# Weight-block sums of the first feed-forward product: from VectorE to GpSimd

## Chip, cores and metric

One core of a Trainium2 chip. The metric is the device time of one execution in microseconds (us); "before" is the median of three runs. The core has TensorE (matrix products), VectorE (DVE in the rows), ScalarE (ACT), GpSimd (POOL) and SyncE (SP, here the queue that issues the loads). TensorE's matmul is PE in the rows, its weight load PEld.

## The reference, cut to what matters

The whole model is two transformer blocks in float32 on 512 tokens of 1024 values. The change touches only the last stage, the feed-forward network of the second block:

```python
def squared_relu_mlp(u, w_ff1, w_ff2):          # u: 512 x 1024, w_ff1: 1024 x 4096, w_ff2: 4096 x 1024
    hdn = jnp.square(jax.nn.relu(jnp.einsum('bld,df->blf', u, w_ff1)))
    return jnp.einsum('blf,fd->bld', hdn, w_ff2)
```

Ahead of it stand the mixer's output projection (w_out), its residual sum and a root-mean-square norm; behind it a residual sum and the final norm.

## The kernel before

**Float32 products from split halves.** A float32 operand is kept as a hi half (rounded by a copy on ScalarE) and a lo half (the rest, a subtraction on VectorE, the helper `rest`, L2059). A product is three matmuls: hi with hi, hi with lo, lo with hi (`mm3`, L614 to L616).

**Units.** The 4096 hidden columns are handled in 16 units of 256 columns, in 4 groups (NFF) of 4. A unit of kind "one" (s = 0 to 15) makes 256 hidden columns; a unit of kind "two" makes 256 output columns from the 1024 hidden columns of one group. The order `SEQ` is: the four "one" units of group 0; then for each further group, alternately "one" of that group and "two" of the group before; last the four "two" units of group 3.

**The first product with seven block products.** A unit "one" is not multiplied straight. The weights of 1024 x 256 are seen as blocks 11, 12, 21, 22 (`squares_of`), the tokens as two halves, and 7 products take the place of 8 (the Strassen-Winograd form). Three of the seven take weight blocks as they are (tiles a and d of a ring), four take sums of blocks: 21+22, that minus 11, 11-21, 12 minus the second. These four sums (tile `sums`, four parts of 128x512) are what the change is about. Before, VectorE makes them in `left_sums` (L2725, L2726, L2727, L2729). ScalarE then copies them to hi halves in two pairs (`s_hi`, L1962), and VectorE makes the lo halves in two pairs (`left_lo`, parts 1 and 2). Part 0 of `left_lo` is the lo half of a and d. TensorE takes the products in the order 1, 2, 6, 5, 7, 3, 4: products 1 and 2 need part 0, 6 and 5 need part 1, 7 and 3 need part 2 (`unit_one`); product 4 takes d.

**Buffers.** Raw weights (1 MB a unit) land in two slots, `raw`, alternating over SEQ. Split halves and sums of a "one" unit lie in a ring: `ring_first` for unit 0, `ring_odd` for units 1 and 3, `ring_even` for all others. So units 1 to 4 have their ring free when product 4 of the unit before the last is done (unit 1: when w_out's last tile is done), while from unit 5 on the ring is free only when product 4 of the unit just before is done. The four sums share their memory with the lo halves `s_lo`. The SyncE queue issues the load of a slot once the splits that read it are done: before, for a "one" unit, after part 0 of `left_lo`.

**VectorE's order, written by hand.** In group 0, in the turn of unit s: first sum of product results (L2784), `left_sums(s+1)`, `left_lo(s+1, 0)`, middle sums (L2790, L2792), lo halves of the hidden tiles of unit s-1, `left_lo(s+1, 1)` and `(s+1, 2)`, last sum (L2797) and the square of the positive part (two scalar_tensor_tensor, L2801). After unit 3 the norm's reciprocal (L2079) and its square. From group 1 on: L2784, `two_lo` (lo halves of a "two" unit), middle sums, hidden lo halves, L2797, L2801, then `left_sums(s+1)` and all of `left_lo(s+1)`, then the residual sums of two "two" tiles (L2820, L2822). ScalarE has a matching order. The last matmul of each product signals `pe_done`; `done(eng, label)` waits for it. GpSimd has no work in the kernel.

The semaphores are counted: `sums_ready` twice a unit before; `w_lo_ready` three times for a "one" unit (`W_AT` holds the base).

Of the kernel before, what the change touches and what calls it, by code (L numbers as in the profile page):

```python
# [25 lines left out]
ALU = mybir.AluOpType  # L26
# [5 lines left out]
KT = D // P  # L32
# [4 lines left out]
RAW = 2  # L37
# [17 lines left out]
NFF = 4  # L55
# [22 lines left out]
U0 = {}  # L78
# [48 lines left out]
SEQ = [("one", 0, u) for u in range(4)]  # L127
# [4 lines left out]
SEQ_AT = {_x: _j for _j, _x in enumerate(SEQ)}  # L132
SPLITS = {"one": 3, "two": 2}
W_AT = [U0["ffn"]]
# [19 lines left out]
def build(nc, t, out):  # L154
    with ExitStack() as ctx:
# [51 lines left out]
        one = vecs[:, NVEC + 1:NVEC + 2]  # L207
# [139 lines left out]
        raw_in = [sem(f"raw_in{i}") for i in range(RAW)]  # L347
# [3 lines left out]
        w_lo_ready = sem("w_lo_ready")  # L351
# [117 lines left out]
        sums_ready = sem("sums_ready")  # L469
# [17 lines left out]
        block = ctx.enter_context(nc.Block())  # L487
# [23 lines left out]
        def odd(s):  # L511
            return s < 4 and s % 2 == 1

        def ring_of(s):
            return ring_first if s == 0 else ring_odd if odd(s) else ring_even
# [10 lines left out]
        def squares_of(u):  # L526

            x = raw[:, u % RAW, :].rearrange("p (i o n) -> p i o n", i=4, o=2)
            return {"a": x[:, :, :, 0:P], "11": x[:, :, 0, 0:P], "12": x[:, :, 1, 0:P],
                    "21": x[:, :, 0, P:2 * P], "22": x[:, :, 1, P:2 * P]}  # L530
# [998 lines left out]
        def done(eng, label):  # L1529

            eng.wait_ge(pe_done, marks.at[label])
            return marks.banks.get(label)


        @block.scalar
        def _(act):
            def split_hi(u):
# [53 lines left out]
            for i in range(4):  # L1591
                u = U0["conv"] + 3 * i
# [363 lines left out]
            def left_sums(s):  # L1956

                r = ring_of(s)
                for i in range(2):
                    act.wait_ge(sums_ready, 2 * s + i + 1)  # L1960
                    c = slice(2 * i, 2 * i + 2)
                    act.activation(r["s"][0][:, c, :, :], r["sums"][:, c, :, :], ACT.Copy).then_inc(w_hi_ready, 1)  # L1962

# [48 lines left out]
            for s in range(4 * NFF):  # L2012
                g, u = divmod(s, 4)
# [34 lines left out]
        def _(dve):  # L2048
            steps = [0]

            def link(ins):

                steps[0] += 1
                ins.then_inc(dve_step, 1)
                dve.wait_ge(dve_step, steps[0])
# [48 lines left out]
            for m in range(KT):  # L2104
                dve.wait_ge(u_hi_ready, m + 1)
                dve.scalar_tensor_tensor(out=C_lo[:, m, :], in0=X[:, m, :], scalar=vec("norm_mix_g", m),  # L2106
                                         in1=C_hi[:, m, :].bitcast(F32), op0=ALU.mult, op1=ALU.subtract)\
# [7 lines left out]
            def latent(m, dst):  # L2115
# [12 lines left out]
                                   in1=vecs[:, g0:g0 + KT].unsqueeze(2).broadcast_to([P, KT, META]), op=ALU.mult))  # L2128
            dve.tensor_tensor(out=meta[:, :, :], in0=meta[:, :, :],
                              in1=meta_sq[:, 0, :].unsqueeze(1).broadcast_to([P, KT, META]), op=ALU.mult)\  # L2130
# [6 lines left out]
            for i in range(4):  # L2137
                u = U0["conv"] + 3 * i
                split_lo(u + 2)
                if i == 0:  # L2140
                    dve.wait_ge(lat_std_ready, 1)
                    link(dve.reciprocal(rstd[:, :], std[:, :]))
                    for k in range(2):
                        dve.scalar_tensor_tensor(out=cqn[:, k, :], in0=cqn[:, k, :], scalar=vec("q_norm_g", k),
                                                 in1=rstd[:, :], op0=ALU.mult, op1=ALU.mult).then_inc(lat_ready, 1)
# [133 lines left out]
            for k in range(KT):  # L2279
                dve.scalar_tensor_tensor(out=memx[:, k, :], in0=memx[:, k, :], scalar=vec("norm_memkv_g", k),  # L2280
                                         in1=rstd[:, 0:MEM], op0=ALU.mult, op1=ALU.mult).then_inc(mem_n_ready, 1)
# [62 lines left out]
            for i in range(4):  # L2344
# [12 lines left out]
                if i < 2:  # L2357
# [8 lines left out]
                                   in1=rstd_t[:, :].unsqueeze(2).broadcast_to([P, TT, EXPERTS]), op=ALU.mult))  # L2366
            link(dve.reduce_max(mx[:, 0:TT], lg, AX_X))
            dve.tensor_tensor(out=aff[:, :, :], in0=lg, in1=mx[:, 0:TT].unsqueeze(2).broadcast_to([P, TT, EXPERTS]),
                              op=ALU.subtract).then_inc(logit_ready, 1)
# [4 lines left out]
                              in1=ri[:, 0:TT].unsqueeze(2).broadcast_to([P, TT, EXPERTS]), op=ALU.mult)\  # L2374
# [8 lines left out]
            for i in range(CAP // 8):  # L2383
# [3 lines left out]
                if i + 1 < CAP // 8:  # L2387
# [9 lines left out]
                              in1=picked[:, :, :], op=ALU.mult).then_inc(pos_ready, 1)  # L2397
# [28 lines left out]
            for p in range(EPAIRS):  # L2426
# [17 lines left out]
                for half in range(2):  # L2444
# [3 lines left out]
                                             in1=YO_hi[:, c].bitcast(F32), op0=ALU.mult, op1=ALU.subtract)\  # L2448
# [72 lines left out]
            for i in range(2):  # L2521
# [5 lines left out]
                              in1=vecs[:, g0:g0 + 2].unsqueeze(2).broadcast_to([P, 2, META]), op=ALU.add)\  # L2527
# [20 lines left out]
            for c in range(2):  # L2548
                dve.wait_ge(z_copied, Z[f"a{4 * c + 3}"])
                for g in (2 * c, 2 * c + 1):  # L2550
# [3 lines left out]
                    for j in range(g + 1):  # L2554
                        dst = win[:, j % 2, :]
                        link(dve.tensor_tensor(out=dst[:, 2 * n - 1:TOK], in0=src[:, 2 * n - 1:TOK],
                                               in1=src[:, n - 1:TOK - n], op=ALU.add))
                        src, n = dst, 2 * n
                    dve.scalar_tensor_tensor(out=AA[:, g, META:TOK], in0=src[:, META:TOK], scalar=1.0 / n,
                                             in1=AA[:, g, META:TOK], op0=ALU.mult, op1=ALU.subtract)\  # L2560
# [10 lines left out]
            for g in range(4):  # L2571
# [3 lines left out]
                                         in1=PH_hi[:, g, :].bitcast(F32), op0=ALU.mult, op1=ALU.subtract)\  # L2575
# [32 lines left out]
            for i in range(4):  # L2608
# [12 lines left out]
                              in0=b[:, :, :, CHUNK - 1:CHUNK].broadcast_to([P, 2, S // CHUNK, CHUNK]), in1=b,  # L2621
                              op=ALU.subtract).then_inc(kd_sub, 1)
            dve.tensor_tensor(out=KD[:, :, 0:META],
                              in0=B2[:, :, META - 1:META].broadcast_to([P, 2, META]), in1=B2[:, :, 0:META],
                              op=ALU.subtract).then_inc(kd_sub, 1)
# [89 lines left out]

            def left_sums(s):

                u = U0["ffn"] + SEQ_AT[("one", s // 4, s % 4)]
                dve.wait_ge(raw_in[u % RAW], 16 * (u // RAW + 1))
                if s == 1:  # L2720
                    done(dve, ("w_out", KT - 1))
                elif s:
                    done(dve, ("p", s - 2 if s < 5 else s - 1, 4))
                x, d = squares_of(u), ring_of(s)["sums"]
                link(dve.tensor_tensor(out=d[:, 0, :, :], in0=x["21"], in1=x["22"], op=ALU.add))  # L2725
                dve.tensor_tensor(out=d[:, 1, :, :], in0=d[:, 0, :, :], in1=x["11"], op=ALU.subtract).then_inc(sums_ready, 1)  # L2726
                dve.tensor_tensor(out=d[:, 2, :, :], in0=x["11"], in1=x["21"], op=ALU.subtract)  # L2727
                dve.wait_ge(sums_ready, 2 * s + 1)
                dve.tensor_tensor(out=d[:, 3, :, :], in0=x["12"], in1=d[:, 1, :, :], op=ALU.subtract).then_inc(sums_ready, 1)  # L2729

            def left_lo(s, part):

                j = SEQ_AT[("one", s // 4, s % 4)]
                r = ring_of(s)
                dve.wait_ge(w_hi_ready, W_AT[j] + part + 1)
                if part == 0:
                    x = squares_of(U0["ffn"] + j)
                    rest(r["a"][1][:, :, :, :], x["a"], r["a"][0][:, :, :, :])
                    rest(r["d"][1][:, :, :], x["22"], r["d"][0][:, :, :]).then_inc(w_lo_ready, 1)
                    return  # L2740
                c = slice(2 * part - 2, 2 * part)
                dve.wait_ge(sums_ready, 2 * s + 2)
                rest(r["s"][1][:, c, :, :], r["sums"][:, c, :, :], r["s"][0][:, c, :, :]).then_inc(w_lo_ready, 1)

            k = SPLIT_NORMS.index("ffn")
# [78 lines left out]
            for s in range(4 * NFF):  # L2824
                g, u = divmod(s, 4)
# [78 lines left out]
        def _(sp):  # L2904
# [24 lines left out]
            u = U0["lat"] + 1  # L2929
# [17 lines left out]
            for i in range(4):  # L2947
                u = U0["conv"] + 3 * i
# [90 lines left out]
            for j, (kind, g, i) in enumerate(SEQ):  # L3039
                u = U0["ffn"] + j  # L3040
                if j < RAW:
                    sp.wait_ge(w_lo_ready, u - RAW + 1)
                else:
                    sp.wait_ge(w_lo_ready, W_AT[j - RAW] + (1 if SEQ[j - RAW][0] == "one" else 2))
                sp.dma_start(dense(raw[:, u % RAW, :]), (ff1 if kind == "one" else ff2)[g, :, :, i * UC:(i + 1) * UC])\
                  .then_inc(raw_in[u % RAW], 16)
            out_v = out.rearrange("(k p) s -> p k s", p=P)
# [69 lines left out]
```

## Time and profile before

| | |
|---|---|
| median of 3 runs | 1905.67 us (1904.06 to 1909.69) |
| profiled execution, its own time | 1904.18 us |
| its span, first to last instruction | 1902.4 us |
| TensorE / VectorE / ScalarE / GpSimd busy | 1844.8 / 940.8 / 592.1 / 0.2 us |
| mean granted TensorE clock | 0.991 |

The feed-forward stage is the span's last fifth, from about 1500 us (output projection and norm) to 1902 us. A row of the timeline gives start, duration, engine, line, operation, what it writes and reads with the shape, and in brackets how long the engine sat idle before it and what it waited for. Neighbouring VectorE operations overlap by some hundredths of a us, so the spacing of starts is the better measure of what a sequence costs.

### The profile page before, as it was taken

Reading aid. Unit: us, or ns where it says so; the run is one execution under the profiler, and the core shown is the slowest. Engines: PE = TensorE matmul, PEld = TensorE weight load, DVE = VectorE, ACT = ScalarE, POOL = GpSimd, SP = SyncE. Lnnn points to the kernel's source line nnn. Section 1 sums busy time; section 2 is a strip of 40 time slices with the busy share of each in tenths; the row PEclk is TensorE's granted clock in tenths of the full one; section 3 lists DMA queues with packets and bytes.
Section 4 is the critical chain, followed back from the end, with each engine's and each line's share of the span. In section 5 each row is a group of like instructions: output and inputs, shape, how many; then the busy total and the mean of one; then the engine's idle time right before and its main releaser. Section 6 shows DMA issues by size and latency. Waiting matters only on the chain.

```text
span 1902.4 us, 22765 instructions
## 1 busy us (share of the span) xinstructions
PE 1844.8 (97%) x9730; PEld 1355.7 (71%) x9730; DVE 940.8 (49%) x1355; ACT 592.1 (31%) x846; POOL 0.2 (0%) x4
## 2 busy tenths in 40 slices
PE   7999999999999999999989998999999999999998
PEld 6788766688898785444433443898888779988998
DVE  6644255533563543011110111656765789777765
ACT  4322334433253421110101101444442344343331
POOL 0000000000000000000000000000000000000000
PEclk9999999999999999999999999999999999999999
DMA  6233211032244417999999999323221223333331
GB/s 185 89 102 97 66 50 37 23 100 100 92 134 133 177 45 313 428 428 428 427 428 428 428 428 372 105 73 89 72 83 45 89 67 112 96 104 103 97 111 45
DMA packets 136852, 324.81 MB, mean 171 GB/s; under 512 B 7456, under 2 KB 119344, under 8 KB 123440
## 3 DMA queue, kind: packets, MB, share of 16 engines
q1 hardware_dynamic: 136752, 323.36, 45.7%
q8 instruction: 77, 1.26, 0.3%
q14 instruction: 23, 0.19, 0.0%
HBM read 321.25 MB, written 2.10 MB: 170 GB/s over the span
## 4 chain that ended last, share of the span: by engine, by line
PE 82%; DVE 7%; DMA 7%; ACT 2%; issue 1%; SPq 0%; DVEq 0%; ACTq 0%
PE bank L614 18%; PE bank L616 17%; PE bank L615 17%; PE bank L1075 12%; DMA ew_f<-in_w_exp_up 3%; DMA ew_b<-in_w_exp_up 2%; DVE w_lo L2059 2%; PE bank L1097 2%; PE bank L1045 2%; PE bank L806 2%; PE bank L782 1%; DMA ew_c<-in_w_exp_up 1%; ACT w_hi L1544 1%; PE bank L1266 1%; PE bank L786 1%
## 5 line engine op out<-in xcount | busy, mean ns | idle before, releaser
L614 PE MATMUL bank<-H_hi,w_hi 128*128 128x512 f32 (+2 forms) x992 | 376.0, 379 | 4.1 <-DVE H_lo L2059 1.8
L615 PE MATMUL bank<-H_lo,w_hi 128*128 128x512 f32 (+2 forms) x992 | 370.5, 373 | 0.0
L616 PE MATMUL bank<-H_hi,w_lo 128*128 128x512 f32 (+2 forms) x992 | 370.4, 373 | 0.0
L2059 DVE TENSOR_TENSOR w_lo<-raw,w_hi 128x2048 fp32r<-128x2048 f32 (+1 forms) x107 | 209.3, 1970 | 221.2 <-ACT w_hi L1544 217.5
L614 PEld LDWEIGHTS bank<-H_hi,w_hi 128*128 128x128 f32 x992 | 186.6, 188 | 54.2 <-issue 14.4
L616 PEld LDWEIGHTS bank<-H_hi,w_lo 128*128 128x128 f32 x992 | 186.6, 188 | 36.1
L615 PEld LDWEIGHTS bank<-H_lo,w_hi 128*128 128x128 f32 x992 | 186.6, 188 | 34.9 <-issue 1.0
L1544 ACT ACTIVATE w_hi<-raw 128x2048 fp32r<-128x2048 f32 x75 | 143.0, 1907 | 138.7 <-PE bank L616 134.8
L2433 DVE SCALAR_TENSOR_TENSOR SG<-bank,gs,SG 128x512 f32<-128x512 f32 x16 | 11.3, 746 | 218.4 <-PE bank L1075 218.4
L1075 PE MATMUL bank<-ew_b,XG 128*64 128x512 f32 x256 | 78.8, 606 | 6.6 <-DMA ew_d<-in_w_exp_up 3.4
L1075 PE MATMUL bank<-ew_c,XG 128*64 128x512 f32 x224 | 78.6, 602 | 0.8 <-DMA ew_c<-in_w_exp_up 0.8
L614 PE MATMUL bank<-C_hi,w_hi 128*128 128x512 f32 x160 | 65.3, 408 | 5.3 <-DVE C_lo L2106 5.3
L1075 PE MATMUL bank<-raw,XG 128*64 128x512 f32 x128 | 58.0, 608 | 6.7 <-DMA ew_f<-in_w_exp_up 6.7
L615 PE MATMUL bank<-C_lo,w_hi 128*128 128x512 f32 x160 | 64.0, 400 | 0.0
L616 PE MATMUL bank<-C_hi,w_lo 128*128 128x512 f32 x160 | 64.0, 400 | 0.0
L1075 PE MATMUL bank<-ew_e,XG 128*64 128x512 f32 x128 | 58.0, 608 | 2.7 <-DMA ew_c<-in_w_exp_up 2.7
L1075 PE MATMUL bank<-ew_f,XG 128*64 128x512 f32 x128 | 58.1, 609 | 1.0 <-DMA ew_a<-in_w_exp_up 1.0
L1800 ACT ACTIVATE AT<-bank 128x512 f32<-128x512 f32 x16 | 9.6, 597 | 156.3 <-PE bank L1084 156.3
L1075 PEld LDWEIGHTS bank<-ew_b,XG 128*64 128x64 f32 x256 | 25.4, 140 | 44.0 <-issue 44.0
L1989 ACT ACTIVATE p<-bank 128x256 f32<-128x256 f32 x42 | 16.1, 384 | 129.4 <-PE bank L616 129.4
L614 PE MATMUL bank<-FF_hi,w_hi 128*128 128x512 f32 x128 | 50.7, 396 | 1.7 <-DVE w_lo L2059 1.7
L615 PE MATMUL bank<-FF_lo,w_hi 128*128 128x512 f32 x128 | 50.6, 396 | 0.0
(536 smaller groups left out, 3700.2 us busy)
## 6 DMA issues: line engine op xcount, KB each, us to landing
raw<-in_w_in SPq DMA_DIRECT2D x38, 1024.0 KB, 5.6
raw<-in_w_ff SPq DMA_DIRECT2D x32, 1024.0 KB, 5.5
ew_b<-in_w_exp_up SPq DMA_DIRECT2D x9, 2048.0 KB, 24.1
ew_c<-in_w_exp_up SPq DMA_DIRECT2D x8, 2048.0 KB, 24.5
ew_b<-in_w_exp_gate SPq DMA_DIRECT2D x7, 2048.0 KB, 30.4
ew_c<-in_w_exp_gate SPq DMA_DIRECT2D x6, 2048.0 KB, 30.8
ew_c<-in_w_exp_down SPq DMA_DIRECT2D x6, 2048.0 KB, 24.4
ew_e<-in_w_exp_gate SPq DMA_DIRECT2D x5, 2048.0 KB, 30.2
```

The lines of the kernel that those rows point to most:

```text
L614: pe.matmul(o, lhs[0], rhs[0], start=first, stop=False, **kw)
L615: pe.matmul(o, lhs[0], rhs[1], start=False, stop=False, **kw)
L616: return pe.matmul(o, lhs[1], rhs[0], start=False, stop=last, **kw)
L782: pe.matmul(o[h][:, :], qn[:, h, c], kn[:, h, :], start=True, stop=False)
L786: mark(pe.matmul(o[h][:, :], qr[r, c], kr[r, :], start=False, stop=True), ("sc", t, h, i))
L806: ins = pe.matmul(bank[7][:, c:c + P], vt[:, h, j, :], pt[:, h, j, :], start=(j == 0), stop=(j == TT - 1))
L1045: ins = pe.matmul(bank[4 + half][:, :], OH[:, tt, :], part[:, tt, half * S:(half + 1) * S], start=(tt == 0 and part is TK_hi), stop=(tt == ...
L1075: ins = pe.matmul(acc[half][r, :], lhs[:, k, r], views[e][:, j, half * S:(half + 1) * S], start=(k == 0), stop=(k == KT - 1))
L1097: ins = pe.matmul(o[:, :], part[:, m * P:(m + 1) * P], OT[:, p % 2, :], start=(part is YO_hi), stop=(part is YO_lo))
L1266: ins = pe.matmul(o[:, i * P:(i + 1) * P], a[r, hp, o0 + cp * P:o0 + (cp + 1) * P], b[r, hp, cp * P:(cp + 1) * P], start=True, stop=True)
L1544: act.activation(w_slot(u, True), raw[:, u % RAW, :], ACT.Copy).then_inc(w_hi_ready, 1)
L2059: return dve.tensor_tensor(out=dst, in0=src, in1=hi_part.bitcast(F32), op=ALU.subtract)
```

## The change

The four sums of a unit are written in a function `block_sums(eng, s)`, which VectorE calls for unit 0 only; GpSimd calls it for units 1 to 15, one after the other, after unit 0's are done. Each sum now signals `sums_ready` (four times a unit), and the two dependences inside (second sum on the first, fourth on the second) are waits for it. ScalarE's and VectorE's waits count accordingly. The load of a raw slot behind a "one" unit now waits for all three lo parts instead of the first.

```diff
+        def block_sums(eng, s):
+            u = U0["ffn"] + SEQ_AT[("one", s // 4, s % 4)]
+            eng.wait_ge(raw_in[u % RAW], 16 * (u // RAW + 1))
+            if s == 1:
+                done(eng, ("w_out", KT - 1))
+            elif s:
+                done(eng, ("p", s - 2 if s < 5 else s - 1, 4))
+            x, d = squares_of(u), ring_of(s)["sums"]
+            eng.tensor_tensor(out=d[:, 0, :, :], in0=x["21"], in1=x["22"], op=ALU.add).then_inc(sums_ready, 1)
+            eng.wait_ge(sums_ready, 4 * s + 1)
+            eng.tensor_tensor(out=d[:, 1, :, :], in0=d[:, 0, :, :], in1=x["11"], op=ALU.subtract).then_inc(sums_ready, 1)
+            eng.tensor_tensor(out=d[:, 2, :, :], in0=x["11"], in1=x["21"], op=ALU.subtract).then_inc(sums_ready, 1)
+            eng.wait_ge(sums_ready, 4 * s + 3)
+            eng.tensor_tensor(out=d[:, 3, :, :], in0=x["12"], in1=d[:, 1, :, :], op=ALU.subtract).then_inc(sums_ready, 1)
+
+        @block.gpsimd
+        def _(pool):
+            pool.wait_ge(sums_ready, 4)
+            for s in range(1, 4 * NFF):
+                block_sums(pool, s)
...
-                    act.wait_ge(sums_ready, 2 * s + i + 1)
+                    act.wait_ge(sums_ready, 4 * s + 2 * i + 2)
...
             def left_sums(s):
-                (the same four tensor_tensor on VectorE, with the same waits)
+                if s == 0:
+                    block_sums(dve, s)
...
-                dve.wait_ge(sums_ready, 2 * s + 2)
+                dve.wait_ge(sums_ready, 4 * s + 4)
...
-                    sp.wait_ge(w_lo_ready, W_AT[j - RAW] + (1 if SEQ[j - RAW][0] == "one" else 2))
+                    sp.wait_ge(w_lo_ready, W_AT[j - RAW] + (3 if SEQ[j - RAW][0] == "one" else 2))
```

## Rows read from the trace of the kernel before

**Rows 1.** The page, busy time, share and instructions of each engine.

```profile
PE 1844.8 (97%) x9730; PEld 1355.7 (71%) x9730; DVE 940.8 (49%) x1355; ACT 592.1 (31%) x846; POOL 0.2 (0%) x4
```

**Rows 2.** Windows of unit 2, unit 3, and one later period; columns in the first line.

```profile
core 0: us, PE busy (x) PEld busy (x) DVE busy (x) ACT busy (x) POOL busy (x), PEclk, DMA share, GB/s
...
1562.00:1573.00 11.00, 11.00 (x95) 11.00 (x94) 8.66 (x14) 5.82 (x10) 0.00 (x0) 1.00 0.27 74
1573.00:1583.00 10.00, 10.00 (x88) 10.00 (x87) 9.90 (x16) 5.83 (x10) 0.00 (x0) 1.00 0.30 99
...
1656.00:1677.00 21.00, 21.00 (x133) 18.82 (x132) 15.66 (x22) 8.06 (x12) 0.00 (x0) 1.00 0.33 101
```

**Rows 3.** TensorE's timeline from group 0's last matmul to the first second-product unit.

```profile
1601.16 0.28 PE L616 MATMUL bank<-TR_hi,ring_even_d_lo 128*128 128x256 f32 x1
1603.18 0.50 PE L614 MATMUL bank<-FF_hi,w_hi 128*128 128x512 f32 x1 [1.74 <-DVE w_lo L2059]
```

**Rows 4.** VectorE's timeline in group 0, from 1575 us to 1603 us.

```profile
1575.27 0.42 DVE L2784 TENSOR_TENSOR T<-bank,p 128x256 f32<-128x256 f32 x1
1575.60 0.68 DVE L2725 TENSOR_TENSOR ring_odd_sums<-raw 128x512 f32<-128x512 f32 x1
...
1578.13 1.22 DVE L2059 TENSOR_TENSOR ring_odd_a_lo<-raw,ring_odd_a_hi 128x1024 fp32r<-128x1024 f32 x1
...
1581.87 2.35 DVE L2059 TENSOR_TENSOR ring_odd_s_lo<-ring_odd_sums,ring_odd_s_hi 128x1024 fp32r<-128x1024 f32 x2
...
1596.33 3.35 DVE L2079 RECIPROCAL rstd<-std 128x512 f32<-128x512 f32 x1
...
1600.78 2.35 DVE L2059 TENSOR_TENSOR w_lo<-raw,w_hi 128x1024 fp32r<-128x1024 f32 x2
```

**Rows 5.** GpSimd's groups of instructions: one of its four.

```profile
L3108 POOL MEMSET const-float32-1.0<- 128x1 f32 x1 | 0.1, 99 | 0.0
```

**Rows 6.** VectorE's timeline in a later period, from 1666 us.

```profile
1666.36 1.30 DVE L2801 SCALAR_TENSOR_TENSOR TS<-TS 128x512 f32<-128x512 f32 x2
1667.57 0.68 DVE L2725 TENSOR_TENSOR ring_even_sums<-raw 128x512 f32<-128x512 f32 x1
...
1670.10 1.22 DVE L2059 TENSOR_TENSOR ring_even_a_lo<-raw,ring_even_a_hi 128x1024 fp32r<-128x1024 f32 x1
...
1671.84 2.35 DVE L2059 TENSOR_TENSOR ring_even_s_lo<-ring_even_sums,ring_even_s_hi 128x1024 fp32r<-128x1024 f32 x2
```

**Rows 7.** ScalarE's timeline: the first second-product unit, and the later period.

```profile
1593.41 2.00 ACT L2010 ACTIVATE w_hi<-raw 128x1024 fp32r<-128x1024 f32 x2
...
1669.01 2.27 ACT L1962 ACTIVATE ring_even_s_hi<-ring_even_sums 128x1024 fp32r<-128x1024 f32 x2 [0.62 <-DVE ring_even_sums L2726]
```

**Rows 8.** TensorE's timeline: products 1, 6, 7 and 4's end, next unit.

```profile
1656.48 0.28 PE L614 MATMUL bank<-C_hi,ring_even_a_hi 128*128 128x256 f32 x1
...
1659.28 0.28 PE L614 MATMUL bank<-TR_hi,ring_even_s_hi 128*128 128x256 f32 x1
...
1662.08 0.28 PE L614 MATMUL bank<-TR_hi,ring_even_s_hi 128*128 128x256 f32 x1
...
1666.17 0.28 PE L616 MATMUL bank<-TR_hi,ring_even_d_lo 128*128 128x256 f32 x1
...
1677.48 0.28 PE L614 MATMUL bank<-C_hi,ring_even_a_hi 128*128 128x256 f32 x1
```

**Rows 9.** The raw slots from 1440 us on: the loads' time to landing.

```profile
DMA to landing us min/median/max: 5.0/5.5/6.7
```

**Rows 10.** Timelines around unit 0: end of w_out, norm work, products.

```profile
1542.71 0.39 PE L616 MATMUL bank<-H_hi,w_lo 128*128 128x512 f32 x1
...
1544.41 0.49 DVE L2757 TENSOR_SCALAR T<-X,vecs 128x512 f32<-128x512 f32 x1
...
1545.73 0.52 PE L614 MATMUL bank<-C_hi,ring_first_a_hi 128*128 128x256 f32 x1 [2.62 <-DVE X L2750]
...
1549.71 0.96 DVE L2059 TENSOR_TENSOR TR_lo<-TR_sums,TR_hi 128x768 fp32r<-128x768 f32 x1
...
1553.00 0.36 PE L614 MATMUL bank<-TR_hi,ring_first_s_hi 128*128 128x256 f32 x1
```

More of the change, by code:

```diff
@@ L2716, in left_sums @@
             def left_sums(s):
[L2718 to L2729, printed above, removed]
+                if s == 0:
+                    block_sums(dve, s)
             def left_lo(s, part):
```

## The prediction

> **What bounds the kernel now.** I read the busy shares first: TensorE is busy 97% of the span, GpSimd 0% [rows 1]. The change can only move TensorE's gaps, so next come the windows of the feed-forward stage: from group 1 on TensorE has no gap at all (21.00 of 21.00 us in each period of one first-product and one second-product unit), while VectorE is at 15.66 of 21; before that, in group 0, VectorE is full, 9.90 of 10.00 us [rows 2]. TensorE's timeline then shows where that fullness reaches it: 1.74 us of gap before the matmul at 1603.18, which waits for the lo half of the first second-product unit; the array had been free since 1601.16 + 0.28 = 1601.44 [rows 3]. VectorE's timeline shows why that half is late: VectorE runs without a break through the sums of units 3 and 4, the reciprocal (3.35 us) and only then the split at 1600.78, which ends at 1603.13 [rows 4]. So the stage is bounded by VectorE up to 1603, and by TensorE after it.
>
> **What the change takes away.** Four tensor_tensor of 128x512 in each of 15 units (1 to 15; unit 0 stays on VectorE). From start to start they take 1578.13 - 1575.60 = 2.53 us [rows 4]; 15 x 2.53 = 38 us leave VectorE. For the 11 units made from group 1 on (5 to 15) this is worth nothing, since TensorE doesn't wait there. The sums of units 3 and 4 are on the chain to 1603.13: 2 x 2.53 = 5.1 us less, but TensorE is free at 1601.44 only, so at most 1603.18 - 1601.44 = 1.74 us come back. That is the largest gain I can find.
>
> **What it adds: GpSimd's operation.** The trace has none of this kind; GpSimd shows only 0.1 us memsets of one column [rows 5]. From below: VectorE's own operation, 0.68 us (less is excluded: the same elements are read and written, and no 128x512 operation of two inputs in the trace is shorter). From above: the slowest 128x512 operation here, the reciprocal's 3.35 us [rows 4]. The nearest row is the same tensor_tensor; I suppose that GpSimd fetches the two operands one after the other, 1024 reads, for which the 128x1024 tensor_tensor at 1670.10 is the row: 1.22 us [rows 6]. Four are 4.9 us, with the two waits inside 5.1 us. The Trainium skill (GPSIMD Engine Reference, section on performance versus the Vector engine) gives 4497 ns for 2048 elements; a quarter of that, an estimate, is 1.12 us, and by it a unit's sums would take 0.4 us less; no run here shows it.
>
> **Where it lies from unit 5 on.** GpSimd starts when product 4 of the unit before is done, 1666.17 + 0.28 = 1666.45 [rows 8], and no longer behind VectorE's two STTs (the scalar_tensor_tensor from 1666.36), after which VectorE started the sums at 1667.57 [rows 6]. Undisturbed it ends at 1666.5 + 5.1 = 1671.6, where VectorE ended at 1670.1. ScalarE's second hi half (the second of the pair at 1669.01 [rows 7]) can start at 1671.6 instead of 1670.1, and the two lo halves of the sums, from 1671.84 before [rows 6], end at 1671.7 + 2.4 = 1674.1, as before. TensorE needs the first part (squares a and d) at 1677.48, the first sums 1659.28 - 1656.48 = 2.80 us later, at 1680.28, and the rest 1662.08 - 1656.48 = 5.60 later, at 1683.08 [rows 8]. Even if the two engines took turns (below), with 0.65 us for an STT, the order STT, sum, STT, sum, a, sum, d, sum would end, step by step, at 1666.95, 1668.2, 1668.8, 1670.1, 1671.3, 1672.5, 1673.2 and 1674.7 (waits included), and the two last lo halves at 1675.9 and 1677.1: the three parts are there 4.3, 4.4 and 6.0 us before they are needed. Cost 0, eleven times. Behind the waiting lo half on VectorE stands the adding of a second-product tile, which TensorE asks for only four tiles later.
>
> The load of the raw slot is issued after the third lo part instead of the first, 2.35 us later (the pair at 1671.84 [rows 6]); nothing else stands behind it on the load queue. It lands 5.5 us after issue [rows 9], so at 1674.2 + 5.5 = 1679.7, with turns at 1682.6; ScalarE reads that slot next some 2 us ahead of 1669.01 + 21 [rows 7], at 1688. In group 0 the tightest is the first second-product load: the lo pair from 1581.87 ends at 1584.2 [rows 4], + 5.5 = 1589.7 against ScalarE's read at 1593.41 [rows 7]. Cost 0. GpSimd's own queue is empty otherwise.
>
> **Where it lies in group 0.** Here VectorE has no room, and nearly all its operations (lo splits, the STTs) read SBUF alone. If the engines are independent, the 1.74 us come back: the lower bound of the cost. If a GpSimd operation and a VectorE operation with two SBUF inputs can't run together and take turns, VectorE loses 4.9 us a unit less what lies beside its reads of PSUM (0.42 us each [rows 4], about two a unit: 0.8), and gains 2.5: +1.6 us for each of units 3 and 4, +3.2 us on the chain to 1603: the upper bound at 1.22 us an operation. Unit 2 is absorbed: VectorE idles 11.00 - 8.66 = 2.3 us in its window [rows 2]. Unit 1's sums now start when the output projection's last tile is done, 1542.71 + 0.39 = 1543.10, beside the norm work for which TensorE already waits 2.62 us before 1545.73 [rows 10]; in VectorE's order they came only after that work. The tensor_scalar at 1544.41 would wait some 0.5 us for the sum in front of it. The rest of that chain ends at 1549.71 + 0.96 = 1550.67 and TensorE wants it at 1553.00 [rows 10]; of 4.9 us in turns 3.3 land on it, less 2.3 us of slack: 1.0. Together +1.5 us. Sum with turns: 3.2 + 1.5 = +4.7 us; without any mutual cost: -1.7.
>
> This is where a rule speaks against the change. The rows show VectorE's operations at 0.68 us with GpSimd silent [rows 4, 5], and cannot show more. The Trainium skill (SBUF — State Buffer, its parts on the engine ports and contention) says that the two engines share a port pair under an exclusive lock, that a VectorE instruction with two SBUF inputs contends with a GpSimd one that reads SBUF, and that whichever comes later blocks fully. By the rule the time would be some 5 us longer, without it 1.7 us shorter. No row here decides.
>
> **Forecast and rivals.** The sum is made on the profiled execution, 1904.18 us (span 1902.4, 1.8 around it). The median of the runs, 1905.67, is 1.5 above it; I leave that in the range, as the runs spread over 1904.06 to 1909.69.
> *Turns (forecast, 0.45):* 1904.2 + 4.7 = 1909 us. Its own range is 1906 to 1913: up to 1.2 more if unit 5's first sum cuts into the split at 1600.78, up to 2 more where unit 4's sums meet the lo halves of unit 3's. For it: both engines stream two operands from the same memory. Against: the trace shows no shared resource.
> *No mutual cost (0.22):* 1904.2 - 1.7 = 1902.5 us. The gap before 1603.18 closes and nothing else moves.
> *Both a little slower (0.23):* GpSimd's 4.9 us cost VectorE half, 2.5, which equals the 2.5 removed; only unit 1 is left, about +1: 1905 us.
> *GpSimd too slow for the repeating part (0.07), the other side:* in 11 units all four sums must be done by 1680.28 - 1.22 = 1679.06, 12.5 us after their start; so it decides from 3.1 us an operation, or from (12.5 - 2.6)/4 = 2.5 us with turns. At the upper bound, 3.35 us, the first sums' lo half is late by 1666.5 + 13.6 + 1.2 - 1680.3 = 1.0 us, with turns by 3.6: 11 x 1.0 to 3.6 is +11 to +40 us, 1915 to 1944. Against it: that bound is a row of another operation.
> *A gain of over 5.7 us (0.03)* would need gaps that I put down to other work, such as the 2.62 us before 1545.73.
>
> A measurement of this kernel tells about 0.3% (5.7 us) from no change, so 1900 to 1911.4 is "same". Of the 0.45 of turns I put 0.20 above it; with the slow GpSimd 0.27 slower, 0.03 faster, 0.70 same. The range leaves out the slow GpSimd, the far gain and the tips of the turns; with the 1.5 of the median on top it is 1902.5 to 1915.
>
> **What would show it.** GpSimd with 60 operations, of 1.22 us by my step, of over 2.5 at the danger point. VectorE or GpSimd operations longer, or further apart, wherever both run: turns; each as alone: no mutual cost. The matmul at 1603.18 about 3 us later and still behind a gap (turns), or 1.7 earlier with none. The first matmul of unit 0 at 1545.73 + 0.5. Periods of 21.00 us from group 1 on; a longer one, with a wait for sums on ScalarE or VectorE that reaches TensorE, would make the prediction wrong upwards, and a shorter chain before 1553 downwards.

## The result, and the profile after

The changed kernel takes 1914.5 us (median of 15 runs, 1906.45 to 1916.67) against 1909.76 us (1903.29 to 1912.61, also 15) for the kernel before: ratio 1.0022, 95% interval 1.0011 to 1.0032. That is about 4 us slower, inside the 0.3% that I had called "same" and near the +4.7 of the forecast. The median of the kernel before is itself 4.1 us above the 1905.67 of the three runs that I had. The profiled execution has a span of 1907.8 us against 1902.4.

Busy time first (the answer to [rows 1]):

```profile
PE 1847.9 (97%) x9730; PEld 1356.3 (71%) x9730; DVE 954.5 (50%) x1295; ACT 592.2 (31%) x846; POOL 104.4 (5%) x64
```

VectorE has 60 instructions fewer and is busy 14 us longer. So its other operations became longer. GpSimd's 60 operations take (104.4 - 0.4) / 60 = 1.73 us each.

TensorE's timeline, the three places of [rows 3, 10]; the number in brackets is the idle time:

```profile
1546.03 0.55 PE L614 MATMUL bank<-C_hi,ring_first_a_hi 128*128 128x256 f32 x1 [3.02 <-DVE X L2762]
...
1587.91 0.58 PE L614 MATMUL bank<-TR_hi,ring_odd_s_hi 128*128 128x256 f32 x1 [3.08 <-DVE ring_odd_s_lo L2081]
...
1608.24 0.51 PE L614 MATMUL bank<-FF_hi,w_hi 128*128 128x512 f32 x1 [0.55 <-DVE w_lo L2081]
```

A new gap of 3.08 us stands in unit 3, ahead of product 6; the gap before the first second-product unit shrank from 1.74 to 0.55. Here are both engines in that stretch, first VectorE (the answer to [rows 4]; pairs are marked x2), then GpSimd:

```profile
1575.55 3.03 DVE L2813 SCALAR_TENSOR_TENSOR TS<-TS 128x512 f32<-128x512 f32 x2
1578.51 0.41 DVE L2796 TENSOR_TENSOR T<-bank,p 128x256 f32<-128x256 f32 x1
1578.84 1.98 DVE L2081 TENSOR_TENSOR ring_odd_a_lo<-raw,ring_odd_a_hi 128x1024 fp32r<-128x1024 f32 x1
...
1582.12 3.53 DVE L2081 TENSOR_TENSOR FF_lo<-TS,FF_hi 128x512 fp32r<-128x512 f32 x2
1585.58 4.50 DVE L2081 TENSOR_TENSOR ring_odd_s_lo<-ring_odd_sums,ring_odd_s_hi 128x1024 fp32r<-128x1024 f32 x2
...
1601.39 3.34 DVE L2101 RECIPROCAL rstd<-std 128x512 f32<-128x512 f32 x1
...
1605.84 2.35 DVE L2081 TENSOR_TENSOR w_lo<-raw,w_hi 128x1024 fp32r<-128x1024 f32 x2
```

```profile
1578.11 1.63 POOL L1549 TENSOR_TENSOR ring_odd_sums<-raw,ring_odd_sums 128x512 f32<-128x512 f32 x1
1582.11 1.29 POOL L1544 TENSOR_TENSOR ring_even_sums<-raw 128x512 f32<-128x512 f32 x1 [2.38 <-PE bank L616]
1583.48 1.62 POOL L1546 TENSOR_TENSOR ring_even_sums<-ring_even_sums,raw 128x512 f32<-128x512 f32 x1
1585.07 1.71 POOL L1547 TENSOR_TENSOR ring_even_sums<-raw 128x512 f32<-128x512 f32 x1
1586.85 2.14 POOL L1549 TENSOR_TENSOR ring_even_sums<-raw,ring_even_sums 128x512 f32<-128x512 f32 x1
```

The two engines take turns. While unit 4's sums run on GpSimd (1582.11 to 1588.99), the pair s_lo of unit 3 takes 4.50 us instead of 2.35 [rows 4], and the pair FF_lo 3.53 instead of the 1.29 that it took in the kernel before:

```profile
1580.65 1.29 DVE L2059 TENSOR_TENSOR FF_lo<-TS,FF_hi 128x512 fp32r<-128x512 f32 x2
```

That is 4.4 us lost. Unit 3's own sums were not late: the last of them ended at 1579.74, ScalarE had their hi halves done at 1582.52, and VectorE came to the lo halves only at 1585.58. The VectorE operation at 1578.51, which reads one operand from PSUM (`bank`), takes its usual 0.41 us in the middle of a GpSimd sum (1578.11 to 1579.74); the next one, which reads two operands from SBUF, ends 1.08 us after that sum. A GpSimd operation that had to wait shows its wait inside its duration (2.14 instead of 1.29).

The gap has a second price, the granted clock (PEclk) in the windows behind it:

```profile
1588.00:1590.00 2.00, 2.00 (x9) 2.00 (x10) 2.00 (x1) 0.00 (x0) 0.99 (x1) 0.50 0.00 0
1590.00:1592.00 2.00, 2.00 (x11) 2.00 (x11) 1.97 (x6) 0.38 (x1) 0.00 (x0) 0.50 0.32 69
1592.00:1594.00 2.00, 2.00 (x12) 2.00 (x12) 2.00 (x4) 0.00 (x0) 0.00 (x0) 0.58 1.07 363
```

After 3.08 us without a matmul, TensorE ran at half clock (1.2 GHz) to about 1594. Unit 3 takes 15.92 us from its first matmul to the next unit's; in two other runs (below), with the same gap and the whole clock behind it, it takes 13.40 and 13.41. The half clock thus cost 2.5 us here.

**A ruler for the experiments.** What lies ahead of the stage differs between executions: in the profiles shown here, unit 0's first matmul comes anywhere from 1544.6 to 1552.5 us, in kernels that are all but the same up to there. So besides the timed ratio I compare two stretches in each profile: A, from unit 0's first matmul to the first matmul of the first second-product unit; and B, from there to the start of the last group's second product (first matmul on the H tiles in the final order). For the kernel before, A = 1603.18 - 1545.73 = 57.45, B = 1845.48 - 1603.18 = 242.30 us. The ratios rest on 12 runs of each experiment, but on 4 with the later sums doubled and on 6 of 7 with tensor_tensor beside it, where one execution (1965.46 us, granted clock 0.913) fell into a slower state and is left out.

| kernel | A | B | largest gaps of TensorE in A | ratio to before (95%) |
|---|---|---|---|---|
| before | 57.45 | 242.30 | 1.74 | |
| changed | 62.21 | 242.31 | 3.08, 0.55 | 1.0022 (1.0011 to 1.0032) |
| GpSimd from unit 5 on | 58.77 | 244.41 | 3.05 | 1.0022 (1.0007 to 1.0036) |
| GpSimd for units 1 to 4 | 60.49 | 242.76 | 3.07, 1.34 | 1.0018 (1.0005 to 1.0030) |
| unit 4 back on VectorE | 59.84 | 245.39 | 3.25 | 1.0023 (1.0008 to 1.0038) |
| units 2 to 4 held back | 61.43 | 243.84 | 1.41, 3.31 | 1.0036 (1.0021 to 1.0052) |
| before, tensor_tensor beside it | 62.57 | 245.03 | 0.94, 1.19, 0.84, 2.87 | 1.0037 (1.0023 to 1.0052) |
| before, 5 memsets beside it | 57.53 | 242.86 | 1.74 | 0.9992 (0.9979 to 1.0005) |
| before, 14 memsets beside it | 57.51 | 244.41 | 1.75 | one execution, not compared |
| before, 5 copies beside it | 59.84 | 242.76 | 0.65, 2.54 | one execution, not compared |
| changed, later sums doubled | 62.25 | 252.44 | 3.09, 0.55 | 1.0067 (1.0050 to 1.0084) |
| before, reciprocal later | 55.58 | 242.20 | none | 0.9990 (0.9976 to 1.0005) |
| from unit 5 on, reciprocal later | 55.49 | 242.20 | none | 0.9978 (0.9959 to 0.9997) |
| changed, reciprocal later | 59.00 | 242.20 | 3.07 | 1.0010 (0.9990 to 1.0031) |

Every run, the kernel before too, has three smaller gaps in A (0.47, 0.47 and 0.78 us), which the table leaves out. In six of the profiles every second period of B is 21.09 us instead of 21.00, some 0.5 us in all. Among them are the two with memsets and the one in which GpSimd has nothing to do after unit 4, so its sums don't cause it; what does stays open. What B holds above that is time at the lower clock behind the gap at its start, save in the run with the sums doubled, where the periods themselves are longer.

### The profile page after: what moved, and what is told of

The parts are those of the page before. It is cut to its first block, busy times and chain, and to the rows that moved or that the text cites. A ratio compares the mean times of both kernels' runs of the same rounds, so it can differ in the third digit from the quotient of the medians.

```text
span 1907.8 us, 22767 instructions
## 1 busy us (share of the span) xinstructions
PE 1847.9 (97%) x9730; PEld 1356.3 (71%) x9730; DVE 954.5 (50%) x1295; ACT 592.2 (31%) x846; POOL 104.4 (5%) x64
## 4 chain that ended last, share of the span: by engine, by line
PE 82%; DMA 7%; DVE 7%; ACT 2%; issue 1%; SPq 0%; DVEq 0%; ACTq 0%
PE bank L614 18%; PE bank L616 18%; PE bank L615 18%; PE bank L1075 12%; DMA ew_f<-in_w_exp_up 3%; DMA ew_b<-in_w_exp_up 2%; DVE w_lo L2081 2%; PE bank L1097 2%; PE bank L1045 2%; PE bank L806 2%; PE bank L782 1%; DMA ew_c<-in_w_exp_up 1%; ACT w_hi L1566 1%; PE bank L1266 1%; PE bank L786 1%
```

## The experiments

My theory: GpSimd's sums and VectorE's operations on two SBUF tensors take turns, and this costs only in group 0, where VectorE has no room. Rivals: the cost is spread over all units; it is the sums' lateness and not the sharing; it is a bound on VectorE's sum of work.

### Is it sharing, and of what?

Four kernels are the one before, with all sums on VectorE, plus GpSimd work that nobody waits for. Only the operation and its count differ:

```diff
+        @block.gpsimd
+        def _(pool):
+            wide = ones[:, :].unsqueeze(1).broadcast_to([P, 3, P])
...
+            for s in range(1, 4 * NFF):
...
+                done(pool, ("w_out", KT - 1) if s == 1 else ("p", s - 2 if s < 5 else s - 1, 4))
+                for i in range(5):
+                    pool.tensor_tensor(out=spare[:, :, :], in0=wide, in1=wide, op=ALU.add).then_inc(idle_step, 1)
+                    pool.wait_ge(idle_step, 5 * (s - 1) + i + 1)
```

With memset: `pool.memset(spare[:, :, :], 1.0)`; with copy: `pool.tensor_copy(out=spare[:, :, :], in_=wide)`.

**tensor_tensor.** 

> The kernel before with all its sums on VectorE, and beside them five operations a unit on GpSimd that nothing waits for: tensor_tensor of 128x384 that reads two SBUF operands (a constant) and writes a spare tile, started where the changed kernel starts its sums. Nothing of the computation is changed. Theory (turns over the reading of SBUF): VectorE's operations with two SBUF inputs that meet one are stretched to 1.3 us and more; its reads of PSUM are not; group 0 is slower than in the changed kernel, as VectorE still has its sums: +5 to +11 us. Rival (the loss came from the sums being late on GpSimd, not from sharing): 0.

**memset, 5 a unit.** 

> As the run beside it, but GpSimd's five operations a unit are memsets of the same spare tile, which read nothing. Theory (it is the reading of SBUF that is shared, not writing): VectorE's tensor_tensor keep their lengths (0.68 and 1.22 us); tensor_scalar may be stretched a little; time that of before within 1 us. Rival (any GpSimd operation holds VectorE up): several us more, in proportion to GpSimd's busy time.

**memset, 14 a unit.** 

> As the run with memsets on GpSimd, but 14 a unit instead of 5, so that GpSimd is busy for 14 x 0.42 = 5.9 us a unit, as long as with the operations that read. Theory (reading is what is shared): 57.5 us from unit 0's first matmul to the first second-product matmul, as before; VectorE's two-input operations keep 0.68 and 1.22 us. Rival (the five memsets were too short to meet anything): operations stretched, over 59 us.

**copy.** 

> As the run with tensor_tensor beside it on GpSimd, but with five copies of 128x384 a unit, which read one SBUF operand. Theory (any reading of SBUF takes the turn for its own length): VectorE's two-input operations are stretched by up to the length of a copy, less than by a tensor_tensor; between 57.5 and 62.6 us from unit 0's first matmul to the first second-product matmul. Rival (only the second operand is shared): 57.5 us, no stretching.

GpSimd's group in the four runs, in this order of operations (5 tensor_tensor, 5 memsets, 14 memsets, 5 copies a unit), one fence each:

```profile
L1546 POOL TENSOR_TENSOR spare<-ones 128x384 f32<-128x384 f32 x75 | 88.8, 1183 | 1742.7 <-PE bank L618 1738.0
```

```profile
L1546 POOL MEMSET spare<- 128x384 f32 x75 | 31.6, 422 | 1783.5 <-PE bank L618 1780.0
```

```profile
L1546 POOL MEMSET spare<- 128x384 f32 x210 | 88.7, 422 | 1738.7 <-PE bank L618 1727.5
```

```profile
L1546 POOL COPY spare<-ones 128x384 f32<-128x384 f32 x75 | 64.8, 864 | 1762.2 <-PE bank L618 1758.5
```

And VectorE's pair s_lo of unit 3, which each time has GpSimd beside it: with tensor_tensor, with 14 memsets, with copies:

```profile
1589.36 3.61 DVE L2073 TENSOR_TENSOR ring_odd_s_lo<-ring_odd_sums,ring_odd_s_hi 128x1024 fp32r<-128x1024 f32 x2
```

```profile
1587.48 2.36 DVE L2073 TENSOR_TENSOR ring_odd_s_lo<-ring_odd_sums,ring_odd_s_hi 128x1024 fp32r<-128x1024 f32 x2
```

```profile
1589.60 2.96 DVE L2073 TENSOR_TENSOR ring_odd_s_lo<-ring_odd_sums,ring_odd_s_hi 128x1024 fp32r<-128x1024 f32 x2
```

So a loss of this size comes without any sum being moved: A is 62.57 with tensor_tensor, 5.1 us more than before, and the ratio of 1.0037 (+7 us) lies in the range that I had given. The 14 memsets keep GpSimd busy for 88.7 us, as long as the tensor_tensor do (88.8), and leave VectorE at 2.36 and A at 57.51, as the 5 memsets left A at 57.53 with a ratio not told apart from 1: it is the reading of SBUF that the two share here. A copy with one operand is enough to stretch VectorE, by less (0.6 against 1.3 us on this pair; A 59.84). Sharing alone is thus enough for such a loss. That the gap in unit 3 isn't lateness of its own sums is shown by the rows above (ready at 1579.74) and by the run below with unit 4's sums back on VectorE. The Trainium skill (SBUF — State Buffer, who interferes with whom) says that a VectorE instruction with two SBUF inputs contends with a GpSimd one that reads SBUF, but not with one that only writes it. These runs agree: 3.61 and 2.96 us with readers, 2.36 with memsets.

### Where is it paid?

**GpSimd from unit 5 on only.** The edit: `on_pool(s)` is `s >= 5`, and VectorE calls `block_sums` for the rest.

```diff
             for s in range(1, 4 * NFF):
-                block_sums(pool, s)
+                if on_pool(s):
+                    block_sums(pool, s)
...
-                if s == 0:
+                if not on_pool(s):
                     block_sums(dve, s)
```

> GpSimd makes the sums of units 5 to 15 only; VectorE keeps units 1 to 4. Theory (turns, paid in group 0 only): no gap of TensorE in the repeating part (periods 21.00 us), the gap before the first second-product unit stays near 1.7 us, time within 2 us of the kernel before (span 1902 to 1904). Rival (a cost spread over all units, or a general cost of GpSimd running): 11/15 of the loss of about 4 us is still there, +3 us.

My expectation was wrong: the ratio is that of all units on GpSimd. But the rival is wrong too: the repeating part from unit 5's products on has no gap, and its periods are 21.00 and 21.09 us as in the run with GpSimd for units 1 to 4 only. Unit 5's first sum starts when product 4 of unit 4 is done (the last matmul before the first second-product unit), and meets that unit's split. VectorE, then TensorE behind it, then its window:

```profile
1606.08 3.43 DVE L2085 TENSOR_TENSOR w_lo<-raw,w_hi 128x1024 fp32r<-128x1024 f32 x2
```

```profile
1609.56 0.62 PE L614 MATMUL bank<-FF_hi,w_hi 128*128 128x512 f32 x1 [3.05 <-DVE w_lo L2085]
```

```profile
1609.60:1622.40 12.80, 12.80 (x48) 10.20 (x49) 10.81 (x13) 2.12 (x2) 4.35 (x3) 0.87 0.36 117
```

The split takes 3.43 instead of 2.35 us: 1.08, one turn. The gap grows by 1.31 (some 0.1 a unit comes from the sums' new form on VectorE, where the fourth sum now waits for the third: in the trace it starts 0.72 us after it instead of 0.60). And the unit behind the gap runs 12.85 us instead of 11.30, the clock at 0.87. The same 12.85 stands in the run with 14 memsets after a gap of 1.75 only, while before, after 1.74, it is 11.30: whether the clock falls after such a gap differs between these executions, and it is worth 1.55 us here. What decides it was not found.

**GpSimd for units 1 to 4 only** (`1 <= s <= 4`). 

> GpSimd makes the sums of units 1 to 4 only. Theory: the whole loss of the change, +4 to +5.4 us, with a gap of about 3 us in unit 3 ahead of product 6. Rival (spread over all units): 4/15 of the loss, +1 us.

The gap in unit 3 is 3.07 us, as foretold. A is 3.0 longer than before, with 0.5 more in B, so in the profile +3.5; the ratio gives +3.4 us, both a little under the +4 that I gave. The interval alone reaches down to the rival's +1; the gap decides. The clock did not fall after this gap. The two halves of the change, each alone, show about the ratio of both together: their losses lie on one chain, and what is lost in unit 3 makes the room for unit 5's turn.

**Unit 4's sums back on VectorE.** 

> As the changed kernel, but unit 4's sums are on VectorE. Theory (unit 4's sums take turns with the lo halves of unit 3's): the 3 us gap in unit 3 is gone, but VectorE is still behind: unit 3's sums in turns cost it some 2 us more than before, unit 4's sums are back, so the gap before the first second-product unit is 2.5 to 4 us instead of 1.74; total +1.5 to +3 us. Rival (the gap in unit 3 comes from unit 3's own sums being late on GpSimd): the gap stays about 3 us and the total +4 or more.

The gap in unit 3 is gone, as the theory says (VectorE's pairs there take their 1.29 and 2.35 us again), and the gap before the first second-product unit is 3.25 us, in the range given. A is +2.4. The whole of it cost more than I expected, since the clock fell after this gap (the unit behind it took 13.92 instead of 11.30 us): +5.5 in A and B together, with a ratio of 1.0023 (+4.4 us). The time alone would fit the rival; the gap in unit 3 speaks against it.

**Units 2 to 4 held back** until the last lo half of the unit before is done:

```diff
+            if 2 <= s <= 4:
+                eng.wait_ge(w_lo_ready, W_AT[SEQ_AT[("one", 0, s - 1)]] + 3)
```

> As the changed kernel, but GpSimd starts the sums of units 2, 3 and 4 only when the last lo half of the unit before is done. Theory (it is the meeting in time that costs): the gap in unit 3 shrinks from 3 us to under 1 us; the turns fall on the scalar_tensor_tensor and the a and d halves behind instead, so part of the loss stays: +1 to +4 us. Rival (the amount of work on GpSimd costs, wherever it is): same loss as the changed kernel, +4 to +5.4 us.

The turns moved, and the loss with them: no gap in unit 3, but 1.41 us ahead of unit 4 and 3.31 ahead of the first second-product unit. The ratio of 1.0036 is +6.9 us, more than the +4 at most that I gave and more than the rival's; in the profile A is 4.0 us longer and B 1.5, the unit behind the gap at the lower clock. So waiting with the sums gains nothing: within group 0 the turns only move, since VectorE has no room there.

### Does room on VectorE make the turns free?

**The kernel before with the reciprocal later:**

```diff
-                if s == 3:
-                    norm_start("ffn")
-                    link(dve.tensor_tensor(out=rstd[:, :], in0=rstd[:, :], in1=rstd[:, :], op=ALU.mult))
...
+                if s == 4:
+                    norm_start("ffn")
+                    link(dve.tensor_tensor(out=rstd[:, :], in0=rstd[:, :], in1=rstd[:, :], op=ALU.mult))
                 if g:
                     second_out(*divmod(2 * (s - 4), 8))
```

> The kernel before, with the norm's reciprocal and its square (4.1 us on VectorE) moved from the end of group 0 to behind unit 5's lo halves. Theory (VectorE's chain in group 0 is the bound up to 1603 us): the gap of 1.74 us before the first second-product unit closes, nothing else moves: -1.7 us. Rival (something else releases that unit, such as its hi half): the gap stays and the time is that of before.

A falls by 1.87 to 55.58 with no gap left; the timed ratio 0.9990 agrees but its interval reaches beyond 1. So 1.7 to 1.9 us is all that relief of VectorE can bring in this stage, the largest gain that I had found.

**GpSimd from unit 5 on, with the reciprocal later.** 

> GpSimd makes the sums of units 5 to 15 only, and the norm's reciprocal and square stand behind unit 5's lo halves. In the run with late units alone, unit 5's first sum met the split of the first second-product unit (3.43 us instead of 2.35) and the gap ahead of it was 3.05 us. Theory (turns cost only where VectorE is late): with 4 us of room the same turns are free: no gap there, from unit 0's first matmul to the first second-product matmul 55.6 us as in the run with the reciprocal moved and nothing on GpSimd, time -1 to -2 us. Rival (GpSimd costs something in the repeating part): periods longer than in the kernel before by more than 0.1 us, 0 to +2 us in all.

The same turns are there and cost nothing; VectorE at the place of the meeting, and TensorE's first matmul of the second product, without a gap:

```profile
1600.44 2.40 DVE L2817 SCALAR_TENSOR_TENSOR T<-T 128x512 f32<-128x512 f32 x2
1602.77 2.31 DVE L2085 TENSOR_TENSOR ring_even_a_lo<-raw,ring_even_a_hi 128x1024 fp32r<-128x1024 f32 x1
1605.01 1.78 DVE L2085 TENSOR_TENSOR ring_even_d_lo<-raw,ring_even_d_hi 128x512 fp32r<-128x512 f32 x1
```

```profile
1600.10 0.40 PE L614 MATMUL bank<-FF_hi,w_hi 128*128 128x512 f32 x1
```

A is 55.49, B 242.20. Timed, it is the only version whose whole interval lies below 1, if barely: 0.9978 (0.9959 to 0.9997), so it beats the kernel before, by more than the 1 to 2 us that I gave. The profile explains 2 of the 4 us, and the interval holds them; GpSimd's part in the gain is nothing that the profile shows, as A and B are those of the version without it, and the two intervals overlap.

**The changed kernel with the reciprocal later.** 

> The changed kernel with the norm's reciprocal and square behind unit 5's lo halves. Theory: the 3.1 us gap in unit 3 stays (it lies ahead of the reciprocal's place), the 0.55 us gap before the first second-product unit goes: from unit 0's first matmul to there 61.6 us against 62.2 in the changed kernel, time +3 to +4.5 us. Rival (the loss comes from VectorE's total chain): the gap in unit 3 goes too and the time is that of before or less.

The gap in unit 3 stays at 3.07 and the second is gone. A is 59.00, shorter than the 61.6 that I gave, since I had taken over the time at half clock: this time the clock stayed whole behind the gap, as this window shows:

```profile
1588.00:1590.00 2.00, 2.00 (x19) 2.00 (x18) 1.97 (x4) 0.38 (x1) 0.00 (x0) 1.00 0.07 11
```

19 matmuls started in two microseconds here, 9 in the same window of the changed kernel. The ratio of 1.0010 (+1.9 us) is under my +3 to +4.5, with an interval over 1 on both sides: not told apart from no loss, nor from the changed kernel's.

### How much room has the repeating part?

**Later sums doubled.**

```diff
+            if s >= 5:
+                for i in range(4):
+                    eng.tensor_tensor(out=d[:, i, :, :], in0=x["21"], in1=x["22"], op=ALU.add).then_inc(twice, 1)
+                    eng.wait_ge(twice, 4 * (s - 5) + i + 1)
```

> As the changed kernel, but each of the units 5 to 15 has four more sums of the same kind on GpSimd ahead of its own, so that a unit's sums take twice as long. Nothing of the result is changed. My step says that all sums must be ready 12.5 us after their start; at 1.65 us an operation eight take 13.2 us and more with turns, so TensorE should wait 1.5 to 4 us in each of 11 periods: +16 to +44 us over the changed kernel, period 22.5 to 25 us. Rival (the repeating part has more room than I worked out): under +5 us.

The period becomes 21.95 us in the later ones: 0.95 more in each, and B is 10.1 us longer than in the changed kernel. That is less than the +16 that I gave and more than the rival's +5. The eight operations end 13.05 us after their start (1718.06 to 1731.11), and the last two of them meet nothing, since VectorE stands waiting for them. But what TensorE waits for is not a lo half. ScalarE's timeline and TensorE's:

```profile
1731.15 1.06 ACT L1989 ACTIVATE ring_even_s_hi<-ring_even_sums 128x1024 fp32r<-128x1024 f32 x1 [1.56 <-POOL ring_even_sums L1554]
1732.11 0.36 ACT L2016 ACTIVATE p<-bank 128x256 f32<-128x256 f32 x1
```

```profile
1732.62 0.36 PE L615 MATMUL bank<-TR_hi,ring_even_s_hi 128*128 128x256 f32 x1 [0.71 <-ACT p L2016]
```

Product 6 of a unit also needs ScalarE's copy of product 1, and that copy stands behind the hi half of the last sums. I had looked at the queue behind the waiting instruction on VectorE, not on ScalarE. With 13.05 us costing a wait of 0.71 (0.95 of period), the point from which it costs is an estimated 12.1 to 12.3 us for a unit's sums, near the 12.5 that I had worked out from the lo half.

## Why the prediction was right, point by point

**The bound, and the largest gain.** Right. VectorE's chain up to 1603 us is the only place where the gain can lie: with 4 us of room in it A is 55.58, 1.87 less than before; I had 1.74.

**GpSimd's operation, 1.22 us.** Alone it is 1.29 us (at 1582.11), and with the wait behind it 1.37 from start to start; a little above both figures that I had weighed (1.22 and 1.12). In turns it is 1.6 to 2.3, which my sum treats separately.

**Turns.** Right, and now shown by the pair of tensor_tensor against memset. I gave this case 0.45 because no row of the kernel before could decide. The rival by which both are a little slower (0.23, VectorE losing 2.5 us a unit) is out: unit 4's sums cost VectorE 4.4 us, a split of 1.22 us that meets a GpSimd sum takes up to 2.32, and an operation with one operand in PSUM isn't longer at all (0.41).

**From unit 5 on: free, eleven times.** Right. The period is 21.00 us. The later period of the changed kernel, VectorE, GpSimd and the window (the answers to [rows 6] and [rows 2]):

```profile
1671.42 2.40 DVE L2813 SCALAR_TENSOR_TENSOR TS<-TS 128x512 f32<-128x512 f32 x2
1673.74 2.32 DVE L2081 TENSOR_TENSOR ring_even_a_lo<-raw,ring_even_a_hi 128x1024 fp32r<-128x1024 f32 x1
1675.98 1.78 DVE L2081 TENSOR_TENSOR ring_even_d_lo<-raw,ring_even_d_hi 128x512 fp32r<-128x512 f32 x1
1679.01 2.36 DVE L2081 TENSOR_TENSOR ring_even_s_lo<-ring_even_sums,ring_even_s_hi 128x1024 fp32r<-128x1024 f32 x2 [1.26 <-POOL ring_even_sums L1549]
```

```profile
1671.66 1.61 POOL L1544 TENSOR_TENSOR ring_even_sums<-raw 128x512 f32<-128x512 f32 x1 [13.75 <-PE bank L616]
1673.34 1.63 POOL L1546 TENSOR_TENSOR ring_even_sums<-ring_even_sums,raw 128x512 f32<-128x512 f32 x1
1674.93 2.28 POOL L1547 TENSOR_TENSOR ring_even_sums<-raw 128x512 f32<-128x512 f32 x1
1677.29 1.62 POOL L1549 TENSOR_TENSOR ring_even_sums<-raw,ring_even_sums 128x512 f32<-128x512 f32 x1
```

```profile
1656.00:1677.00 21.00, 21.00 (x134) 18.80 (x133) 16.55 (x19) 8.06 (x12) 7.10 (x5) 1.00 0.33 101
```

The order STT, sum, STT, sum, a, sum, d, sum is the one I wrote down (an STT is a scalar_tensor_tensor). TensorE's next unit starts at 1682.55, so a and d (done at 1677.76) are 4.8 us early, where I had 4.3, and the last lo half (1681.37, needed at 1682.55 + 5.60) 6.8 where I had 6.0.

**Group 0, units 3 and 4: +3.2.** The mechanism was right, the place and the size were not. I put the loss on the chain to the gap at 1603. The first to run out was the lo half of unit 3's sums, with unit 4's sums in its way: a gap of 3.08 us there, of which 1.19 came back at the next gap (1.74 to 0.55). That is +1.89 in gaps. I had named this meeting, but as up to 2 us on top of the range, not as the main term. The 0.8 us a unit that I took off for VectorE's reads of PSUM was there for unit 3's sums, but not for unit 4's, where VectorE was behind and had no such read between 1582.12 and 1590.00.

**The clock: no term.** A grew by 4.76 us. The gaps are 1.89 of it and unit 0 is 0.1; of the 2.8 left, all in unit 3 behind its gap, 2.5 are the half clock, and 0.3 stand there with the whole clock too. With the whole clock A was 59.00 and 60.49. So the sum of +4.7 came out for other reasons in part: group 0 in gaps 1.9 instead of 3.2, unit 1 0.5 instead of 1.5 (below), and 2.5 for a clock that I had left out. That the total is near is partly luck.

**The range.** Luck too: 1914.5 us lies 0.5 us under its upper end, and above the 1906 to 1913 that I gave for turns. My sum started from 1904.2, and the median of the kernel before turned out to be 1909.76. The difference of the two kernels was foretold well; the time itself was not.

**Unit 5's first sum cutting into the split.** In the changed kernel it didn't: the loss in unit 3 had already delayed product 4 of unit 4, from whose end GpSimd starts (the matmul at 1601.16 of [rows 3] is this one, not group 0's last), and VectorE had caught up. In the run with the late units alone it did, at the 1.08 that I had as 1.2.

**Unit 1 and the norm work: +1.5.** Too large; measured 0.5 (0.4 ahead of unit 0, 0.1 in it). GpSimd's first sum and VectorE in the norm's chain:

```profile
1543.19 1.73 POOL L1544 TENSOR_TENSOR ring_odd_sums<-raw 128x512 f32<-128x512 f32 x1 [1542.75 <-PE bank L616]
```

```profile
1544.42 0.78 DVE L2769 TENSOR_SCALAR T<-X,vecs 128x512 f32<-128x512 f32 x1
...
1546.64 1.38 DVE L2771 TENSOR_TENSOR TR_sums<-T 128x256 f32<-128x256 f32 x1
1548.05 1.39 DVE L2772 TENSOR_TENSOR T<-T 128x256 f32<-128x256 f32 x1
...
1552.08 0.95 DVE L2081 TENSOR_TENSOR TR_lo<-TR_sums,TR_hi 128x768 fp32r<-128x768 f32 x1
```

The tensor_scalar lost 0.3 (I had 0.5), and the gap ahead of unit 0 grew from 2.62 to 3.02. Four sums cost VectorE only some 2.4 us to the end of the chain (1552.08 against 1549.71), not 3.3, and the slack of 2.3 took nearly all of it: the next unit's start moved by 0.1 us beyond that.

**The slow GpSimd.** It didn't come about, as the periods of 21.00 us show. Its threshold was right within 0.4 us for a unit's sums, but the release that fails first is ScalarE's, not the lo half.

**The slot's later release.** No wait for a load appeared in group 0 or in the repeating part, as worked out; ScalarE's two waits for one at the end of the stage are those of before (10.30, and 1.14 against 1.11 us).

## What to carry to other kernels

Work moved off a full engine to an idle one isn't free if both read SBUF: ask, for every operation that will run beside it, how many SBUF tensors it reads, and count up to one whole operation of the other engine for each meeting. Look for the stretch where the engine to be relieved has no room, since both the gain and the price live only there; in this kernel the cheaper relief was to move 4 us of VectorE work that nobody needed yet. And for each wait that becomes longer, look at what is queued behind it on every engine that waits, not only on the one under study.

## What the runs showed that I had not expected

- A GpSimd memset of 128x384 takes 0.42 us, a copy 0.86 and a tensor_tensor 1.18 in the mean, meetings included. Only those that read stretch VectorE's two-input operations.
- The wait of a turn is counted inside the operation that waits, on either engine: a pair of VectorE operations showed 4.50 instead of 2.35 us, and GpSimd's own 2.14 instead of 1.29. So busy shares overstate the work in such a stretch.
- A VectorE tensor_scalar of one SBUF tensor was stretched as well beside GpSimd's sums (0.78 and 0.64 us instead of 0.49), and not beside memsets (0.49).
- The same gap of TensorE, 3.07 to 3.08 us, was followed by half clock in the changed kernel (2.5 us lost) and by full clock in two others; after 1.74 to 1.75 us it was 11.30 us in one unit and 12.85 in another. What decides between the two stays open.
